# Small constant products on TensorE around the normed output stages of a two-model forward pass

## The chip, the cores and the metric

The kernel runs on one core of a Trainium2 chip. The metric is device time in microseconds of one execution. All arithmetic is float32 in and out; most products are made of three products of split halves.

## The reference

A first block (attention with compressed, selected and windowed keys, a retention branch, a squared-ReLU MLP) is followed by a two-layer model: layer 0 has an mLSTM mixer and layer 1 a softmax attention with forget gates (here "fox"), each followed by a convolved, gated feed-forward part. All on 512 rows of width 1024. The second model is where the change sits:

```python
def rmsnorm_2(x, w):
    xf = x.astype(jnp.float32)
    y = xf * lax.rsqrt(jnp.mean(xf * xf, axis=-1, keepdims=True) + EPS)
    return (y * w.astype(jnp.float32)).astype(x.dtype)

for layer in range(DEPTH_2):
    h = rmsnorm_2(x, norm_mix_pre[layer])
    y = mlstm_mixer(...) if layer < N_A_LAYERS else fox_mixer(...)
    x = x + rmsnorm_2(y, norm_mix_post[layer])
    h = rmsnorm_2(x, norm_ffn_pre[layer])
    y = conv_ffn(h, ...)
    x = x + rmsnorm_2(y, norm_ffn_post[layer])
    if layer == N_A_LAYERS - 1:
        k_sh, v_sh, c_sh = shared_kv(x, kv_norm, kv_w, kv_b_f)
```

There are four places of the form `x = x + rmsnorm_2(y, ...)`: after the mLSTM mixer, after feed-forward 0, after the fox mixer and after feed-forward 1. After each of the first three comes another norm of the new x and a projection of it.

## The kernel before, in words

Everything is kept transposed: x is eight tiles (KT = 8) of 128 features by 512 rows in `xT`. A projection (`dense`, L401) streams its weights in blocks through two slots; ScalarE rounds a block to its high part (L304), VectorE makes the low part (L313), and TensorE does three products per tile (`three_products`, L356 to L360, or tile by tile at L436, L437 and L441 in `by_tile`). Products are 128x128 by 128x512.

`run` (L362) takes a list of stages and makes one block of them: each engine goes through its own part of all stages in order, and at the end of the block every engine drains and takes part in a barrier (those instructions carry L365). The next `run` starts behind it.

The last thing in the block of each normed output stage is `post_root` (L739). The output tiles y have been squared and added on the way (`sums_on_the_way`, L691). In `post_root`, TensorE waits for the sum of seven squares and makes column means of it (`column_sums`, L570, instructions at L574), waits for the eighth square and adds its column sums; ScalarE takes the root of the 128x4 result (L754), VectorE the reciprocal (L758), and TensorE spreads the reciprocals over all partitions into `bank[6]` (`spread`, L578, instructions at L581). VectorE waits for the spread. Then the block ends.

The next block begins with `update_and_split` (L775; for feed-forward 0, fox and feed-forward 1) or, after the last stage, with `update_and_store` (L822), which has no part for TensorE. In both, VectorE scales each y tile by gain and root (`scale_tile`, L768) and adds it to `xT` (`add_tile`, L773). In `update_and_split`, ScalarE then makes the high half of the tile (L585) and its square (L788), VectorE the low half (L589), and TensorE takes the tile into the first block of the next projection (`by_tile`), with the column sums of the tile before it behind each tile's products (`sums`, called by `with_tile`, L809). The feed-forward projections have two chunks, six products for each tile; the fox one (`ff`) has one chunk, three products. ScalarE's square of tile k waits for the column sums of tile k-2, and behind the square of tile 3 ScalarE rounds the second weight block before it goes on to tile 4.

`ident_b` and `bias_b` are 128x128 bf16 constants, made at the start; the attention adds its causal bias with one product of the two at L1092.

Of the kernel before, what the change touches and what calls it, by code (L numbers as in the profile page):

```python
# [13 lines left out]
P = 128  # L14
# [165 lines left out]
def build(nc, io, at):  # L180
    top = ExitStack()
    with top:
        def sb(ctx, name, shape, dt=F32):
            return ctx.enter_context(nc.sbuf_tensor(name, shape, dt))
# [13 lines left out]
        ident_b = sb(top, "ident_b", [P, P], BF16)  # L198
        bias_b = sb(top, "bias_b", [P, P], BF16)
# [12 lines left out]
        bank = [top.enter_context(nc.psum_tensor(f"bank{i}", [P, 512], F32)) for i in range(8)]  # L212
# [357 lines left out]
        def column_sums(pe, col, src, first, last):  # L570


            for t in range(TT):
                ins = pe.matmul(bank[7][:, col + t:col + t + 1], src[:, t * P:(t + 1) * P], mean_of[:, 0:1],  # L574
                                start=first and t == 0, stop=last and t == TT - 1)
            return ins

        def spread(pe, dst, col):  # L578

            for t in range(TT):  # L580
                ins = pe.matmul(dst[:, t * P:(t + 1) * P], col[:, t:t + 1].broadcast_to([P, P]), ident, start=True, stop=True)  # L581
            return ins

        def high(act, k, vec):
            act.activation(a_hi[:, k, :], xT[:, k, :], ACT.Copy, scale=vec(k)).then_inc(split_hi_done.sem, 1)  # L585

        def low(dve, k, vec, b_hi):
            dve.wait_ge(split_hi_done.sem, b_hi + k + 1)
            dve.scalar_tensor_tensor(a_lo[:, k, :], xT[:, k, :], vec(k), a_hi[:, k, :].bitcast(F32),  # L589
                                     ALU.mult, ALU.subtract).then_inc(split_lo_done.sem, 1)  # L590

        def halves_ready(b_hi, b_lo):
            return lambda k: ((split_hi_done.sem, b_hi + k + 1), (split_lo_done.sem, b_lo + k + 1))

        def split_gained(vec):

            b_hi, b_lo, b_pr = split_hi_done.n, split_lo_done.n, products_done.n

            def scalar(act):
                act.wait_ge(products_done.sem, b_pr)  # L600
                for k in range(KT):
                    high(act, k, vec)

            def vector(dve):
                for k in range(KT):
                    low(dve, k, vec, b_hi)
            split_hi_done.n += KT
            split_lo_done.n += KT
            return {"scalar": scalar, "vector": vector}, halves_ready(b_hi, b_lo)

        def pre_root():

            b_s, b_r, b_i, b_sp = sums_ready.n, root_ready.n, inv_ready.n, spread_ready.n

            def act_part(act):
                act.wait_ge(sums_ready.sem, b_s + 1)
                act.activation(inv_col[:, :], bank[7][:, 4:4 + TT], ACT.Sqrt, bias=EPS).then_inc(root_ready.sem, 1)

            def dve_part(dve):
                dve.wait_ge(root_ready.sem, b_r + 1)  # L620
                dve.reciprocal(inv_col[:, :], inv_col[:, :]).then_inc(inv_ready.sem, 1)
                dve.wait_ge(spread_ready.sem, b_sp + 1)
                dve.tensor_copy(inv[:, :], bank[5][:, :])
                dve.drain()

            def pe_part(pe):
                pe.wait_ge(inv_ready.sem, b_i + 1)
                spread(pe, bank[5], inv_col).then_inc(spread_ready.sem, 1)
            for t in (sums_ready, root_ready, inv_ready, spread_ready):
                t.n += 1  # L630
            return act_part, dve_part, pe_part
# [107 lines left out]
        def post_root():  # L739

            b_sum, b_sq = summed.n, squared.n
            b_s, b_r, b_i, b_sp = sums_ready.n, root_ready.n, inv_ready.n, spread_ready.n

            def tensor(pe):
                pe.wait_ge(summed.sem, b_sum)
                column_sums(pe, 0, total, True, False)
                pe.wait_ge(squared.sem, b_sq)
                column_sums(pe, 0, sq[1], False, True).then_inc(sums_ready.sem, 1)
                pe.wait_ge(inv_ready.sem, b_i + 1)
                spread(pe, bank[6], post_col).then_inc(spread_ready.sem, 1)  # L750

            def scalar(act):
                act.wait_ge(sums_ready.sem, b_s + 1)
                act.activation(post_col[:, :], bank[7][:, 0:TT], ACT.Sqrt, bias=EPS).then_inc(root_ready.sem, 1)  # L754

            def vector(dve):
                dve.wait_ge(root_ready.sem, b_r + 1)
                dve.reciprocal(post_col[:, :], post_col[:, :]).then_inc(inv_ready.sem, 1)  # L758
                dve.wait_ge(spread_ready.sem, b_sp + 1)
            for t in (sums_ready, root_ready, inv_ready, spread_ready):  # L760
                t.n += 1
            return {"tensor": tensor, "scalar": scalar, "vector": vector}

        def scale_tile(dve, src, vec, k, b_sc, b_up):

            if k >= 2:
                dve.wait_ge(updated.sem, b_up + k - 1)
            dve.scalar_tensor_tensor(y_part[k % 2][:, :], src[:, k, :], gain(vec, k), bank[6][:, :],  # L768
                                     ALU.mult, ALU.mult).then_inc(scaled.sem, 1)

        def add_tile(dve, k, b_sc):
            dve.wait_ge(scaled.sem, b_sc + k + 1)
            dve.tensor_tensor(xT[:, k, :], xT[:, k, :], y_part[k % 2][:, :], ALU.add).then_inc(updated.sem, 1)  # L773

        def update_and_split(src, vec, pre):  # L775


            b_sc, b_up, b_hi, b_lo, b_sq, b_sum = scaled.n, updated.n, split_hi_done.n, split_lo_done.n, squared.n, summed.n
            act_root, dve_root, pe_root = pre_root()
            b_s = sums_ready.n - 1  # L780

            def ahead_act(act, second_block):
                for k in range(KT):
                    act.wait_ge(updated.sem, b_up + k + 1)
                    high(act, k, pre)
                    if k >= 2:
                        act.wait_ge(summed.sem, b_sum + k - 1)
                    act.activation(sq[k % 2][:, :], xT[:, k, :], ACT.Square).then_inc(squared.sem, 1)  # L788
                    if k == 3:
                        second_block()  # L790
                act_root(act)

            def ahead_dve(dve, second_block):
                for k in range(KT):
                    scale_tile(dve, src, vec, k, b_sc, b_up)
                    if k >= 1:
                        dve.wait_ge(updated.sem, b_up + k)
                        low(dve, k - 1, pre, b_hi)
                    add_tile(dve, k, b_sc)
                dve.wait_ge(updated.sem, b_up + KT)  # L800
                low(dve, KT - 1, pre, b_hi)
                second_block()
                dve_root(dve)

            def sums(pe, k):
                pe.wait_ge(squared.sem, b_sq + k + 1)
                column_sums(pe, 4, sq[k % 2], k == 0, k == KT - 1).then_inc(sums_ready.sem if k == KT - 1 else summed.sem, 1)

            def with_tile(pe, k):  # L809
                if k >= 1:  # L810
                    sums(pe, k - 1)
                if k == KT - 1:
                    sums(pe, k)
            scaled.n += KT
            updated.n += KT
            split_hi_done.n += KT
            split_lo_done.n += KT
            squared.n += KT
            summed.n += KT - 1
            return dict(ahead_act=ahead_act, ahead_dve=ahead_dve, tile_ready=halves_ready(b_hi, b_lo), with_tile=with_tile), pe_root  # L820

        def update_and_store(src, vec):  # L822
# [1214 lines left out]
        def post_norm(name, y, src=None):  # L2037

            early_dve, late_dve, late_act, count = sums_on_the_way(y, copied(y))
            stages, ready = [], None  # L2040
            if src is not None:
                stage, ready = split_tiles(src, a_hi, a_lo, KT)
                stages.append(stage)
            stages.append(dense(name, two_chunks(a_tiles), early_dve, late_dve, none, late_act, tile_ready=ready))
            count()
            run(*stages, post_root())
# [216 lines left out]
```

## Time and profile before

| | us |
|---|---|
| median of 3 runs (lowest, highest) | 2392.88 (2389.38, 2394.75) |
| the profiled execution | 2392.39 |
| its span | 2390.5 |
| mean granted TensorE clock | 0.943 |
| TensorE busy with products | 2184.3 (91%) |
| VectorE busy | 1236.5 (52%) |
| ScalarE busy | 827.9 (35%) |

The profiled execution is 1.9 us longer than its span, the time from the first to the last instruction. The granted clock is a share of 2.4 GHz: 1.0 is 2.4 GHz and 0.5 is 1.2 GHz; no other level is granted, and a mean between them is a mix.

### The profile page before, as it was taken

How to read it: one execution, taken by the hardware profiler on the slowest of the kernel's cores; microseconds unless marked ns; L12 is line 12 of the kernel's file. 1: busy time of each engine (PE TensorE's matmuls, PEld its weight loads, DVE VectorE, ACT ScalarE, POOL GpSimd, SP SyncE). 2: the span in 40 equal slices, each digit the busy share in tenths (PEclk: the TensorE clock that was granted, in tenths of full speed). 3: DMA queues.
4: the chain of work that ended last, by engine and by line, in shares of the span. 5: the costliest groups of instructions: out<-in, count | busy, mean ns of one | idle time of the engine just before them, and what ended most of it. 6: DMA issues, size and time to landing. Idle time of an engine off the chain costs nothing. (4 is left out here: it accounts for less than half of the span.)

```text
span 2390.5 us, 27004 instructions
## 1 busy us (share of the span) xinstructions
PE 2184.3 (91%) x10048; PEld 1752.7 (73%) x10048; DVE 1236.5 (52%) x1760; ACT 827.9 (35%) x1202; POOL 25.4 (1%) x50
## 2 busy tenths in 40 slices
PE   7878888999999998798699999997998789999997
PEld 6645666887888887676578888876886467888885
DVE  4566444445443455324557465556344655747465
ACT  4146214433222123224435233333124654524232
POOL 0000000000000000002000000001000000000000
PEclk9868998999999999898799999996999999999998
DMA  5200211232222321221112223212221011222221
GB/s 170 78 1 1 106 44 53 83 118 88 88 98 96 106 88 62 89 88 53 36 54 106 104 88 106 84 49 88 88 88 53 1 55 69 96 99 92 101 88 53
DMA packets 33848, 185.85 MB, mean 78 GB/s; under 512 B 4024, under 2 KB 8280, under 8 KB 14176
## 3 DMA queue, kind: packets, MB, share of 16 engines
q1 hardware_dynamic: 32608, 182.57, 21.7%
q10 hardware_dynamic: 1152, 2.10, 0.3%
q8 instruction: 56, 0.92, 0.2%
q14 instruction: 32, 0.26, 0.0%
HBM read 182.54 MB, written 2.11 MB: 77 GB/s over the span
## 5 line engine op out<-in xcount | busy, mean ns | idle before, releaser
L358 PE MATMUL bank<-a_hi,w_hi 128*128 128x512 f32 x1504 | 591.4, 393 | 29.1 <-DVE w_lo L313 23.3
L304 ACT ACTIVATE w_hi<-w_raw 128x2048 fp32r<-128x2048 f32 (+3 forms) x171 | 313.8, 1836 | 875.0 <-PE bank L360 771.5
L359 PE MATMUL bank<-a_lo,w_hi 128*128 128x512 f32 x1504 | 588.9, 392 | 0.0
L360 PE MATMUL bank<-a_hi,w_lo 128*128 128x512 f32 x1504 | 588.6, 391 | 0.0
L313 DVE TENSOR_TENSOR w_lo<-w_raw,w_hi 128x2048 fp32r<-128x2048 f32 (+3 forms) x171 | 374.9, 2193 | 191.1 <-ACT w_hi L304 191.0
L358 PEld LDWEIGHTS bank<-a_hi,w_hi 128*128 128x128 f32 x1504 | 284.8, 189 | 90.1 <-DVE w_lo L313 24.6
L360 PEld LDWEIGHTS bank<-a_hi,w_lo 128*128 128x128 f32 x1504 | 284.7, 189 | 59.9
L359 PEld LDWEIGHTS bank<-a_lo,w_hi 128*128 128x128 f32 x1504 | 284.9, 189 | 58.7
L358 PE MATMUL bank<-w_hi,a_hi 128*128 128x512 f32 (+1 forms) x288 | 111.2, 386 | 6.3 <-DVE w_lo L313 2.7
L360 PE MATMUL bank<-w_hi,a_lo 128*128 128x512 f32 (+1 forms) x288 | 109.7, 381 | 0.0
L359 PE MATMUL bank<-w_lo,a_hi 128*128 128x512 f32 (+1 forms) x288 | 109.6, 381 | 0.0
L358 PE MATMUL bank<-ffn_hi,w_hi 128*128 128x512 f32 x264 | 103.4, 392 | 3.0 <-DVE w_lo L313 3.0
L359 PE MATMUL bank<-ffn_lo,w_hi 128*128 128x512 f32 x264 | 102.8, 389 | 0.0
L360 PE MATMUL bank<-ffn_hi,w_lo 128*128 128x512 f32 x264 | 102.7, 389 | 0.0
L2085 DVE TENSOR_TENSOR ffn_u<-bank,inv 128x512 f32<-128x512 f32 x88 | 56.7, 687 | 79.6 <-PE bank L360 78.9
L436 PE MATMUL bank<-a_hi,w_hi 128*128 128x512 f32 x112 | 53.0, 473 | 36.7 <-ACT a_hi L585 14.0
L2073 ACT ACTIVATE ffn_z<-ffn_u,conv 128x512 f32<-128x512 f32 x88 | 66.5, 803 | 26.7 <-DVE ffn_u L2085 26.7
L358 PE MATMUL bank<-mlp_hi,w_hi 128*128 128x512 f32 x192 | 74.7, 389 | 0.0
L359 PE MATMUL bank<-mlp_lo,w_hi 128*128 128x512 f32 x192 | 74.7, 389 | 0.0
L360 PE MATMUL bank<-mlp_hi,w_lo 128*128 128x512 f32 x192 | 74.7, 389 | 0.0
L2076 ACT ACTIVATE ffn_z<-ffn_z 128x512 f32<-128x512 f32 x44 | 27.9, 634 | 120.8 <-DVE ffn_z L2095 120.8
L358 PEld LDWEIGHTS bank<-w_hi,a_hi 128*128 128x128 f32 x288 | 54.8, 190 | 19.2 <-issue 4.1
(367 smaller groups left out, 3016.9 us busy)
## 6 DMA issues: line engine op xcount, KB each, us to landing
w_raw<-in_w_fu SPq DMA_DIRECT2D x44, 1024.0 KB, 4.8
w_raw<-in_w_up SPq DMA_DIRECT2D x16, 1024.0 KB, 4.9
w_raw<-in_w_down SPq DMA_DIRECT2D x16, 1024.0 KB, 4.8
w_raw<-in_w_fd SPq DMA_DIRECT2D x16, 1024.0 KB, 4.8
w_raw<-in_w_mix SPq DMA_DIRECT2D x8, 1024.0 KB, 4.8
w_raw<-in_w_fd SPq DMA_DIRECT2D x8, 768.0 KB, 4.3
w_raw<-in_w_rqk SPq DMA_DIRECT2D x4, 1024.0 KB, 4.9
w_raw<-in_w_rvg SPq DMA_DIRECT2D x4, 1024.0 KB, 4.8
```

Source lines behind the costliest of these rows:

```text
L304: act.activation(w_hi[slot][:, 0:n], raw[slot][:, 0:n], ACT.Copy).then_inc(hi_ready.sem, 1)
L313: dve.tensor_tensor(w_lo[slot][:, 0:n], raw[slot][:, 0:n], w_hi[slot][:, 0:n].bitcast(F32), ALU.subtract).then_inc(lo_ready.sem, 1)
L358: pe.matmul(out, w[0], x[0], start=first, stop=False)
L359: pe.matmul(out, w[0], x[1], start=False, stop=False)
L360: return pe.matmul(out, w[1], x[0], start=False, stop=last)
L436: pe.matmul(bank[2 * slot + c][:, :], w[0], x[0], start=k == 0, stop=False)
L2073: act.activation(z[slot][:, c, :], u[slot][:, c, 2:S + 2], ACT.Identity, scale=tap(2, b, c), bias=tap(3, b, c)).then_inc(tapped.sem, 1)
L2076: act.activation(z[slot][:, 0, :], z[slot][:, 0, :], ACT.Gelu_apprx_tanh).then_inc(gelu_ready.sem, 1)
L2085: ins = dve.tensor_tensor(u[slot][:, c, 2:S + 2], bank[2 * slot + c][:, :], inv[:, :], ALU.mult)
```

## The change

A helper `keep_busy` issues n products of `ident_b` with `bias_b` (128x128 by 128x128, bf16) into `bank[4]`, which nobody reads at that point. They wait for nothing and signal nothing. `post_root` issues 7 of them between the column sums and the wait for the reciprocals, and 32 behind the spread; this is in all four normed output stages. `update_and_split` issues 12 behind the products of tile 0, in the three stages that have it. In all 4 x 39 + 3 x 12 = 192 products, each with its own weight load.

```diff
+        def keep_busy(pe, n):
+
+            for _ in range(n):
+                pe.matmul(bank[4][:, 0:P], ident_b[:, :], bias_b[:, :], start=True, stop=True)
+
@@ post_root, tensor(pe)
                 column_sums(pe, 0, total, True, False)
                 pe.wait_ge(squared.sem, b_sq)
                 column_sums(pe, 0, sq[1], False, True).then_inc(sums_ready.sem, 1)
+                keep_busy(pe, 7)
                 pe.wait_ge(inv_ready.sem, b_i + 1)
                 spread(pe, bank[6], post_col).then_inc(spread_ready.sem, 1)
+                keep_busy(pe, 32)
@@ update_and_split
             def with_tile(pe, k):
                 if k >= 1:
                     sums(pe, k - 1)
+                elif k == 0:
+                    keep_busy(pe, 12)
                 if k == KT - 1:
                     sums(pe, k)
```

## Rows read from the trace of the kernel before

**Rows 1.** The page: busy time by engine, and the granted clock in 40 slices
```profile
PE 2184.3 (91%) x10048; PEld 1752.7 (73%) x10048; DVE 1236.5 (52%) x1760; ACT 827.9 (35%) x1202; POOL 25.4 (1%) x50
...
PEclk9868998999999999898799999996999999999998
```

**Rows 2.** Timeline (start, duration in us) of the output stage after the mLSTM
```profile
1223.02 0.39 PE L360 MATMUL bank<-a_hi,w_lo 128*128 128x512 f32 x1
...
1225.70 1.65 PE L574 MATMUL bank<-mean_of,sq 128*128 128x1 f32 x8
...
1227.38 0.17 ACT L754 ACTIVATE post_col<-bank 128x4 f32<-128x4 f32 x1 [2.59 <-PE bank L574]
...
1227.82 2.08 PE L581 MATMUL bank<-const_sb,post_col 128*128 128x128 f32 x8 [0.47 <-DVE post_col L758]
```

**Rows 3.** Source view of L365, 1227 to 1232 us: ns min/median/max, first to last start
```profile
L365 PEldq EVENT_SEMAPHORE  x2: 51/51/51, 1230.0 to 1230.4; - x2
L365 DVEq EVENT_SEMAPHORE  x2: 21/21/21, 1230.2 to 1230.4; - x2
L365 POOLq EVENT_SEMAPHORE  x2: 17/17/17, 1230.3 to 1230.3; - x2
L365 PEldq DRAIN  x1: 2103/2103/2103, 1227.8 to 1227.8; - x1
```

**Rows 4.** Timeline: the first instructions behind that barrier
```profile
1230.63 0.75 DVE L768 SCALAR_TENSOR_TENSOR y_part<-y,gains,bank 128x512 f32<-128x512 f32 x1 [2.87 <-POOL ffn_u L2059]
...
1232.14 0.72 ACT L585 ACTIVATE a_hi<-xT,gains 128x512 fp32r<-128x512 f32 x1 [4.58 <-DVE xT L773]
...
1233.01 0.76 PE L436 MATMUL bank<-a_hi,w_hi 128*128 128x512 f32 x1 [3.11 <-ACT a_hi L585]
```

**Rows 5.** Windows, TensorE alone: stretch, length, busy (count), granted clock, DMA share, GB/s
```profile
1222.50:1225.50 3.00, 1.62 (x11) 1.00 0.00 0
...
1226.00:1232.50 6.50, 3.42 (x15) 0.50 0.12 21
...
1236.00:1236.50 0.50, 0.50 (x3) 0.82 0.00 0
```

**Rows 6.** Source view of L1092, the same product in the attention
```profile
L1092 PE MATMUL bank<-bias_b,ident_b x128: 219/219/314, 142.7 to 1932.9; 128*128 128x128 bf16 x128
```

**Rows 7.** Timeline of two such pairs (the first product alone, then both), and their clocks
```profile
142.74 0.29 PE L1092 MATMUL bank<-bias_b,ident_b 128*128 128x128 bf16 x1
...
142.74 0.40 PE L1092 MATMUL bank<-bias_b,ident_b 128*128 128x128 bf16 x2
...
1932.86 0.28 PE L1092 MATMUL bank<-bias_b,ident_b 128*128 128x128 bf16 x2
...
142.50:143.50 1.00, 1.00 (x10) 0.50 0.00 0
1932.50:1933.50 1.00, 1.00 (x8) 1.00 0.00 0
```

**Rows 8.** Timeline: tiles 3 and 4 of feed-forward 0's first projection
```profile
1240.59 0.63 ACT L788 ACTIVATE sq<-xT 128x512 f32<-128x512 f32 x1 [1.04 <-PE bank L574]
...
1241.13 1.89 ACT L304 ACTIVATE w_hi<-w_raw 128x2048 fp32r<-128x2048 f32 x1
...
1243.68 0.50 PE L436 MATMUL bank<-a_hi,w_hi 128*128 128x512 f32 x1 [0.86 <-ACT a_hi L585]
```

**Rows 9.** Timeline, then windows, of the fox projection's tiles
```profile
1617.39 0.80 PE L441 MATMUL bank<-a_lo,w_hi 128*128 128x512 f32 x1 [1.21 <-DVE a_lo L589]
...
1620.44 0.79 PE L436 MATMUL bank<-a_hi,w_hi 128*128 128x512 f32 x1 [2.25 <-ACT a_hi L585]
...
1639.38 0.77 PE L436 MATMUL bank<-a_hi,w_hi 128*128 128x512 f32 x1
...
1620.00:1644.00 24.00, 23.09 (x85) 0.50 0.08 26
...
1649.00:1650.00 1.00, 1.00 (x9) 0.90 0.00 0
```

## Prediction

> **What bounds the kernel now.** I read the page first: TensorE is busy 91% of the span, and its granted clock is at the full 2.4 GHz in most slices with short dips [rows 1]. So the kernel is bound by TensorE, and what is left to gain lies where it waits or runs at 1.2 GHz. The change touches four such places. I then read the timeline of the one after the mLSTM, the source view of the block end, and the clock in windows; the other three show the same pattern to a few hundredths of a microsecond.
>
> The order of events there: the last dense product starts at 1223.02; the column sums of the last square start at 1225.70; the root starts at 1227.38; the spread starts at 1227.82 and lasts 2.08 us [rows 2]. TensorE's clock is still full up to 1225.5 and is at half from 1226.0, so the sums of the last square and the spread run at 1.2 GHz [rows 5]. It rises again inside 1236.0 to 1236.5, some 3 us after the first dense products of the next projection began at 1233.01 [rows 4, 5].
>
> What matters most is what stands between the spread and the next work. TensorE's queue has a DRAIN of 2.103 us that begins at 1227.8 and so ends at 1229.9, with the spread. Its barrier semaphore follows at 1230.0, VectorE's at 1230.2, GpSimd's at 1230.3 [rows 3]. Only behind that barrier does VectorE scale the first tile, at 1230.63, ScalarE makes its high half at 1232.14 and TensorE starts on it at 1233.01 [rows 4]. The source view shows the same 2.103 us drain at all three places where another projection follows, and at the last place too. So whatever TensorE has in its queue ahead of the block's end holds up every engine, and VectorE's chain behind the barrier is the critical path: TensorE itself is idle for 3.11 us waiting for it [rows 4].
>
> **The change part by part.**
>
> *The price of one product.* The kernel already has the same product, one at a time 0.219 us long at the full clock [rows 6]. Two in a row last 0.28 us at the full clock, so the second adds 0.06; at half clock one lasts 0.29 and two 0.40, so the second adds 0.11 [rows 7]. I take 0.11 and 0.06. Only pairs are in the trace: if a longer row did not overlap at all, each would cost up to the 0.31 us of the longest single one [rows 6], which I hold for unlikely, since a pair overlaps.
>
> *7 products behind the column sums.* They come after the clock has fallen, so they can't keep it up. They fill the 0.47 us in which TensorE waits for root and reciprocal [rows 2]: 7 x 0.11 = 0.77 us. The last column sum starts about 0.35 us before its end, so the products get perhaps 0.15 us more than the gap. Bounds per place: 0 (all hidden) and 0.3 (nothing but the gap). I take 0.15; four places, 0.6 us.
>
> *32 products behind the spread.* These stand ahead of the block's DRAIN. The cover would be the wait of 3.11 us for the first tile, but that wait only begins when the barrier is through: the products don't lie beside it, they push it back. 32 x 0.11 = 3.5 us, if the clock stays at half. Off that go 0.2 us, the time by which TensorE's semaphore is ahead of VectorE's now [rows 3], and some 0.3 us because TensorE is then continuously busy for over 5 us and the clock, which rose about 3 us after dense work began [rows 4, 5], should rise near the end of the row. That leaves 3.0 us at each of four places, 12.0 us. Bounds: all 32 at the full clock, 32 x 0.06 - 0.2 = 1.7 us, and all at half with no rise, 3.5 - 0.2 = 3.3 us; times four, 6.8 and 13.2.
>
> *What the risen clock brings.* After the products TensorE waits again, now for barrier, two VectorE and one ScalarE instruction: 1229.9 to 1233.01, 3.1 us, unchanged in length. The trace shows that the clock fell within 2.6 us after the last dense product, although the first column sums lay in that time [rows 2, 5]. An idle wait of 3.1 us should lose it again, before or about when tile 0 arrives. Then tiles 0 and 1 run at 1.2 GHz as now. Gain taken: 0. If the clock is full for tile 0: TensorE is late in this stretch, ScalarE's square of tile 3 waits 1.04 us for its column sums, the weight block is rounded behind that, and tile 4 starts on TensorE behind both [rows 8]. With a full clock nearly all of that goes; about 0.9 us at each of the two feed-forward stages.
>
> The Trainium skill ("TensorE: Matmul & The Clock Gate", section on HAM oscillation) says that bursts of products with waits between them start at the low clock again each time, because the clock is released by recent activity and throttled by recent idleness. By that rule the 32 products buy a clock which the wait behind them gives back. No row here shows such a burst of small products; if the page's opposite advice, keep TensorE busy before dense work, decided instead, the sum would be that of the rival "clock is kept" below.
>
> *12 products behind tile 0.* In the feed-forward stages, TensorE goes from tile 0 to tile 1 with no wait at half clock, so 12 products cost up to 12 x 0.11 = 1.3 us there, less what an earlier rise of the clock or a later wait takes back (ScalarE's waits for sums pass a delay on to tile 4). Bounds: -0.9 us (clock full, the products in a gap, the gain above) and +1.3 us. I take 0.4 at each of two stages, 0.8 us. In the fox stage they are hidden: TensorE waits 2.25 us before tile 1 [rows 9], because VectorE is slow there.
>
> *Sum.* 0.6 + 12.0 + 0.8 = 13.4 us on the profiled execution's 2392.39 (span 2390.5 and 1.9 outside it) gives 2405.8. The median of the runs is 0.5 above the profiled one, so 2406.
>
> **The rivals.**
>
> *The clock is not down when the products come.* The time that passes before the clock falls need not be the same at every place once the first one has moved the rest. If it stays full through sums and spread at a place, the spread costs about 1 us less and the 32 products only 1.7 us: about +1 us there. If this held at three of four places: 3.2 + 3 x 1 = 6, less up to 1.8 at the tiles, some +4 us, 2397. For it: the fall now comes right inside the sums, a small shift could move it. Against: all four places of before, hundreds of microseconds apart, fall at the same point.
>
> *The clock is kept (not slower).* If the products raise the clock early and it survives the wait, the fox stage decides: now its clock is at half from the output stage to 1649 us [rows 9]; tiles 1 to 7 start 18.94 us apart in all, 3.2 us a tile, and at the full clock VectorE's three instructions a tile, 0.75 us for the longest [rows 4], some 2.2 in all, would set the pace. Six tiles give 5.6 us; of the ten us from 1639.4 until the clock has risen at 1649.5, all TensorE's at half clock, I estimate that a third would go, 3.4, so 9 us; with 1.8 in the feed-forward stages that is 11 against 4 x 1.7 + 0.6 = 7.4: -3.5 us, 2389. Its place is the fox projection, its price 9 us, and it decides if the clock is full when tile 1 of fox arrives. Against it: after tile 0 in fox TensorE has waits of over 1 and over 2 us between few products [rows 9], and 12 products of 0.06 cover 0.7 of them.
>
> *The drain does not hold the others.* If the 32 products ran beside the barrier, they would end about when tile 0 arrives and cost nothing, the clock would be up for the feed-forward tiles: -1.8 + 0.6, down to -10 with fox: 2382 to 2391. Against it stands the 2.103 us DRAIN that ends with the spread [rows 3].
>
> **How the numbers follow.** The sum as worked out 0.78, clock not down 0.12, clock kept 0.05, drain doesn't hold 0.05. The likeliest gives 2406; its own range is 2398 to 2410: 6.8 us less 1.8 at the tiles is +5, and 13.2 with 1.2 and 2.6 for the other two parts is +17. For 8 in 10 I go down into the first rival and up for products that overlap less than the pairs do: 2397 to 2411. A measurement of this kernel tells 0.2%, 4.8 us, from no change. Slower by more: the likeliest case and a part of the first rival, 0.82. Within: the rest of the first rival and most of the clock kept, 0.12. Faster: 0.06.
>
> **What would show it.** In the profile after, the DRAIN of TensorE in front of each of the four barriers is some 5.3 us long in place of 2.1; VectorE's first scaling starts 3 us later after the reciprocal than now; the last place shows the same loss though no product follows it. The 32 products take 3 to 3.5 us, most at 0.5. The clock is at half when tile 0's products start, and fox's tiles still run at half to the end. The prediction is wrong if the scaling follows the spread as soon as before, if the products run at 0.06 us each, or if the fox tiles run at the full clock.

## The result, and the profile after

The changed kernel takes 2405.86 us (median of 12 runs, 2403.59 to 2416.74), the kernel before 2392.35 (median of 12, 2389.38 to 2401.11): ratio 1.0060, 95% interval 1.0044 to 1.0077. It is 13.5 us slower; 13.4 had been forecast on the profiled execution.

The profiled execution of the changed kernel is a long one, 2416.27 us with a span of 2414.5. Of the 24 us by which its span exceeds the one before, 8.25 were there before the first changed instruction ran: the first output stage's root starts at 1235.63, before at 1227.38 [rows 2]. A second profile of the same program (below, `changed_again`) has that root at 1226.09 and a span of 2403.3. So I measure from root to root and not from the span's start; what the 8.25 us consist of is in the last section. The page of the first profile, to be held against [rows 1]:

```profile
PE 2210.7 (92%) x10240; PEld 1772.8 (73%) x10240; DVE 1236.3 (51%) x1760; ACT 827.8 (34%) x1202; POOL 25.4 (1%) x50
```

TensorE has its 192 more products, and nothing else in the counts has moved. The page alone doesn't tell where the time went. The timeline of the first output stage does (start, duration in us, what; idle time ahead of it in brackets), against [rows 2, 4]:

```profile
1235.46 0.55 PE L587 MATMUL bank<-bias_b,ident_b 128*128 128x128 bf16 x7
1235.63 0.17 ACT L761 ACTIVATE post_col<-bank 128x4 f32<-128x4 f32 x1 [1.97 <-PE bank L574]
...
1236.07 2.08 PE L581 MATMUL bank<-const_sb,post_col 128*128 128x128 f32 x8
1237.94 2.66 PE L587 MATMUL bank<-bias_b,ident_b 128*128 128x128 bf16 x32
...
1241.15 0.75 DVE L775 SCALAR_TENSOR_TENSOR y_part<-y,gains,bank 128x512 f32<-128x512 f32 x1 [5.14 <-POOL ffn_u L2068]
...
1242.66 0.72 ACT L590 ACTIVATE a_hi<-xT,gains 128x512 fp32r<-128x512 f32 x1 [6.86 <-DVE xT L780]
...
1243.53 0.77 PE L436 MATMUL bank<-a_hi,w_hi 128*128 128x512 f32 x1 [2.93 <-ACT a_hi L590]
```

The 32 products stand between the spread and the first scaling. The spread is over by 1238.15, yet VectorE scales only at 1241.15, half a microsecond behind the last product, and TensorE then waits 2.93 us for tile 0, as it waited 3.11 before. The source view of the block's end in the same stretch (ns min/median/max, first to last start), against [rows 3]:

```profile
L365 DVEq EVENT_SEMAPHORE  x2: 21/21/21, 1238.5 to 1240.9; - x2
L365 PEldq EVENT_SEMAPHORE  x2: 51/51/51, 1240.7 to 1240.9; - x2
L365 PEldq DRAIN  x1: 1170/1170/1170, 1239.5 to 1239.5; - x1
```

TensorE's drain ends at 1240.7, behind the last product's end at 1240.60, and its semaphore follows at once. VectorE had reached its own semaphore at 1238.5, so it stood at the barrier for 2.2 us until TensorE came; before, TensorE's semaphore at 1230.0 was ahead of VectorE's at 1230.2 [rows 3]. The granted clock over the same stage, in windows of TensorE alone (stretch, length, busy, clock, DMA share, GB/s), against [rows 5]:

```profile
1235.50:1236.00 0.50, 0.50 (x8) 1.00 0.00 0
1236.50:1239.00 2.50, 2.50 (x18) 0.50 0.00 0
1239.50:1240.00 0.50, 0.50 (x13) 1.00 0.00 0
1240.00:1242.50 2.50, 0.60 (x11) 1.00 0.10 13
1243.00:1249.00 6.00, 5.47 (x22) 0.50 0.38 158
1249.50:1250.00 0.50, 0.50 (x5) 0.84 0.00 0
```

The products did raise the clock, between 1239.0 and 1239.5. Then TensorE was idle until 1243.53, and the clock was at half again when tile 0 arrived; it came back six microseconds into the tiles. In that time stand the 12 products and what follows from them:

```profile
1246.23 1.50 PE L587 MATMUL bank<-bias_b,ident_b 128*128 128x128 bf16 x12
...
1250.94 0.63 ACT L795 ACTIVATE sq<-xT 128x512 f32<-128x512 f32 x1 [3.12 <-PE bank L574]
...
1256.34 0.50 PE L436 MATMUL bank<-a_hi,w_hi 128*128 128x512 f32 x1 [0.86 <-ACT a_hi L590]
```

They ran at half clock and held tile 1 back until 1247.49; ScalarE's square of tile 2 waited 3.12 us for column sums, and tile 4 starts 15.19 us behind the first scaling, before 13.05 [rows 4, 8].

The same intervals at all places and in all kernels that were run, one profile each, worked out from the timelines (us, each from start to start; the four places are the output stages after the mLSTM, feed-forward 0, fox, feed-forward 1):

| kernel | root to first scaling, the four | scaling to tile 4's high half, ffn 0 and 1 | scaling to tile 7's, fox | root to root | last root to end |
|---|---|---|---|---|---|
| before | 3.25 3.05 3.25 3.05 | 12.29 12.37 | 24.49 | 382.18 382.20 382.16 | 16.58 |
| changed | 5.52 5.14 6.33 5.71 | 14.43 13.15 | 24.47 | 385.99 387.17 386.47 | 19.24 |
| changed_again | 6.36 5.73 6.26 5.65 | 13.15 13.16 | 24.48 | 386.49 385.11 386.47 | 19.14 |
| only_32 | 6.40 6.23 6.17 6.23 | 12.38 12.40 | 24.48 | 385.20 386.68 385.02 | 19.77 |
| only_12 | 3.25 2.13 3.19 3.06 | 12.99 14.00 | 24.48 | 382.38 383.55 383.54 | 16.61 |
| only_7 | 3.28 3.09 3.28 3.09 | 12.30 12.38 | 24.48 | 382.22 382.24 382.20 | 16.59 |
| moved_32 | 3.28 2.22 3.28 3.07 | 13.61 12.26 | 24.46 | 383.03 381.07 381.62 | 16.65 |
| double_32 | 8.15 5.46 7.77 7.05 | 11.60 12.85 | 24.49 | 385.86 386.35 386.68 | 20.62 |
| before_sums | 2.33 3.05 3.25 3.05 | 13.00 13.13 | 24.49 | 381.40 381.96 382.45 | 16.54 |
| all_gaps | 2.34 2.13 3.25 2.46 | 11.61 12.33 | 24.48 | 380.03 383.37 381.64 | 15.97 |
| fox_fill | 2.34 2.24 2.33 2.14 | 11.59 11.63 | 21.86 | 380.08 374.21 380.00 | 15.69 |
| fox_only | 3.25 3.05 3.25 3.05 | 12.34 12.38 | 21.85 | 382.20 375.45 382.14 | 16.56 |

The first three columns are the stages themselves. A root to root holds some 350 us of other work besides, in which the granted clock dips at other moments in each execution, and the middle one moves most by it. The changed kernel has 387.17 there in one profile and 385.11 in the other, though the first of the two had the shorter time from the second root to the first scaling (5.14 us against 5.73). In only_12, from the first scaling to the third root, TensorE is busy 338.42 us at a mean clock of 0.92, before 335.24 at 0.93. So a difference of 1 or 2 us in the middle column, in a single profile, isn't to be read as an effect.

### The profile page after: what moved, and what is told of

Read it like the earlier page. It is cut to its first block and busy times, and to the rows that moved or that the text cites. A ratio compares the mean times of both kernels' runs of the same rounds, so it can differ in the third digit from the quotient of the medians.

```text
span 2414.5 us, 27388 instructions
## 1 busy us (share of the span) xinstructions
PE 2210.7 (92%) x10240; PEld 1772.8 (73%) x10240; DVE 1236.3 (51%) x1760; ACT 827.8 (34%) x1202; POOL 25.4 (1%) x50
```

## The experiments

The theory: TensorE's drain and the barrier at the block's end wait for all that TensorE has been given, so 32 products ahead of it are paid in full at four places. The rivals: the 12 products are the larger cost; the 192 products cost wherever they stand; the clock is what decides. Medians are of 4 to 12 runs of each kernel beside 29 runs of the kernel before, but fox_only and changed_again ran once.

### Each part alone

```diff
 # only_32: the 7 and the 12 are taken out
-                keep_busy(pe, 7)
...
-                elif k == 0:
-                    keep_busy(pe, 12)
```

> Only the 32 products behind the spread, no 7 and no 12. Theory (the drain at the block's end holds every engine): from the root to the first scaling 5.2 to 6.3 us in place of 3.05 to 3.25 at each of four places, the tiles behind it paced as before, in all +9 to +12 us on the median of the kernel before. Rival 1 (the 12 products behind tile 0 are the larger cost): under +5 us. Rival 2 (the products run beside the barrier): the time from root to scaling stays at 3.2 us, and the total at that of before.

Measured 2405.01 us against 2392.3, ratio 1.0055 (1.0041 to 1.0069): 12.7 us, nearly the whole loss, from the 32 alone, and slightly more than the 9 to 12 expected. From root to scaling 6.17 to 6.40 us, 12.4 us more than before at the four places together. Its timeline at the first place, then its clock in windows:

```profile
1228.93 3.54 PE L587 MATMUL bank<-bias_b,ident_b 128*128 128x128 bf16 x32
...
1233.03 0.75 DVE L774 SCALAR_TENSOR_TENSOR y_part<-y,gains,bank 128x512 f32<-128x512 f32 x1 [6.01 <-POOL ffn_u L2065]
...
1235.40 0.53 PE L436 MATMUL bank<-a_hi,w_hi 128*128 128x512 f32 x1 [2.92 <-ACT a_hi L590]
```

```profile
1232.00:1235.00 3.00, 0.48 (x6) 0.96 0.35 44
1235.50:1236.00 0.50, 0.50 (x2) 0.67 1.08 459
1236.00:1239.00 3.00, 3.00 (x8) 0.50 0.41 175
```

Here one sees the purchase and its loss: the clock is full from about 1232 to 1235.5, in which TensorE has next to nothing to do. It falls just when tile 0 has started: its first product still lasts 0.53 us, before 0.76 [rows 4], and everything in the three microseconds behind runs at half. Tile 4 gains nothing by it (12.38 us, before 12.29). The last stage is the cleanest place of all, since no product follows it: last root to end 19.77 us in place of 16.58.

```diff
 # only_12: the 7 and the 32 are taken out
-                keep_busy(pe, 7)
...
-                keep_busy(pe, 32)
```

> Only the 12 products behind tile 0. Theory: they are run at half clock and push tile 1 back; ScalarE's squares pass that on, so in the two feed-forward stages tile 4 comes 0.7 to 2.1 us later after the first scaling than the 12.3 us of before, in fox not at all; in all +1.5 to +4 us. Rival (the products raise the clock for the tiles, as they are meant to): tile 4 at 12.3 us or earlier, total the same or a little less.

Measured 2394.74 us, ratio 1.0004 (0.9992 to 1.0016), which can't be told from no change. The profile can: tile 4 is 0.70 and 1.63 us later than before in the two feed-forward stages, and fox's tiles are where they were. That is within what the theory expected. At the first place the 12 themselves last 1.03 us, at the other two 1.50. One root to scaling is 2.13 us and its spread 1.16 us long: the clock had not fallen there yet, which gives part of the cost back.

```diff
 # only_7: the 32 and the 12 are taken out
-                keep_busy(pe, 32)
...
-                elif k == 0:
-                    keep_busy(pe, 12)
```

> Only the 7 products between column sums and spread. Theory: 0.15 us at each of four places, from root to scaling 3.2 to 3.4 us, total within 1 us of before. Rival (they also keep the clock up for the spread): the spread lasts 1.05 us in place of 2.08 at one or more places, total 1 to 4 us less.

Measured 2391.79 us, ratio 1.0001 (0.9987 to 1.0014). From root to scaling 0.03 to 0.04 us more than before, at all four places.

```profile
1225.27 0.91 PE L587 MATMUL bank<-bias_b,ident_b 128*128 128x128 bf16 x7
1225.45 0.17 ACT L760 ACTIVATE post_col<-bank 128x4 f32<-128x4 f32 x1 [2.55 <-PE bank L574]
...
1225.97 2.02 PE L581 MATMUL bank<-const_sb,post_col 128*128 128x128 f32 x8
```

The spread starts 0.52 us behind the root in place of 0.44 and is 0.06 shorter. Neither a cost nor a clock.

### The same 32, behind the barrier

```diff
 # moved_32
                     tiles = len(sets[0])
+                    if with_tile is not None:
+                        with_tile(pe, -1)
...
-                keep_busy(pe, 32)
...
             def with_tile(pe, k):
+                if k == -1:
+                    keep_busy(pe, 32)
```

> The change whole, but with the 32 products behind the barrier, ahead of the wait for tile 0, in the three stages that have it. Theory (the barrier makes the cost): from root to scaling back to 3.2 to 3.4 us; tile 0 starts on TensorE at most 1 us late if the products run at half clock (32 x 0.107 = 3.4 us against 2.4 us of waiting), and the clock is full at tile 0 or 1. In all -2 to +3 us against before, 10 us or more under the changed kernel. Rival (192 more products and their instructions cost wherever they stand): within 3 us of the changed kernel.

Measured 2391.41 us, ratio 0.9999 (0.9985 to 1.0013), 14 us under the changed kernel: 0.9 less than the kernel before that ran beside it, where the changed one took 13.5 more. This tells the theory from the rival of "wherever they stand", as 96 of the 128 products are still there (the last stage has no tiles for its 32). Its timeline:

```profile
1228.61 0.75 DVE L776 SCALAR_TENSOR_TENSOR y_part<-y,gains,bank 128x512 f32<-128x512 f32 x1 [2.90 <-POOL ffn_u L2071]
1228.63 3.57 PE L589 MATMUL bank<-bias_b,ident_b 128*128 128x128 bf16 x32 [0.75 <-PEq L365]
...
1231.96 0.77 PE L438 MATMUL bank<-a_hi,w_hi 128*128 128x512 f32 x1
```

Scaling and products now start together. At half clock the products outlast the wait: tile 0 starts 3.35 us behind the first scaling, before 2.38 [rows 4], its first product is still at half clock (0.77 us), and with the 12 behind it tile 4 comes 1.32 us later than before. At the other two places the clock rose during the row: tile 0 starts at 3.05 and 3.06 us and its first product lasts 0.48 and 0.47. So the move takes the cost at the drain away, and what is left of it at the tiles is about made up elsewhere (root to scaling of 2.22 us at one place).

### Twice as many

```diff
 # double_32: only these, and 64
-                keep_busy(pe, 32)
+                keep_busy(pe, 64)
```

> Only the products behind the spread, but 64. Theory (all that stands ahead of the drain is paid): the second 32 run at the full clock, 0.056 us each, so 1.8 us more than with 32 alone at each of four places: root to scaling 7.9 to 8.3 us, +7 us against 32 alone. Rival (the cost is a fixed one of a risen clock or of a longer program): the same as with 32 alone.

Measured 2409.08 us, ratio 1.0079 (1.0051 to 1.0107): 4 us more than with 32 (4.6 if each is taken against the kernel before that ran beside it), where 7 were expected. The cost grows with the number, as for work that is paid, but less than forecast. At the first place it is the sum expected:

```profile
1227.79 5.29 PE L587 MATMUL bank<-bias_b,ident_b 128*128 128x128 bf16 x64
...
1233.64 0.75 DVE L774 SCALAR_TENSOR_TENSOR y_part<-y,gains,bank 128x512 f32<-128x512 f32 x1 [7.77 <-POOL ffn_u L2065]
...
1236.02 0.47 PE L436 MATMUL bank<-a_hi,w_hi 128*128 128x512 f32 x1 [2.93 <-ACT a_hi L590]
```

At the second, all ran at the full clock (spread 1.16 us, the 64 products 3.74, root to scaling 5.46), and at the other two it rose earlier in the row (4.91 and 4.45 us). The expected 7 us had the first 32 cost as much as in only_32, mostly at half clock, everywhere. And at the first the clock lived through the wait: tile 0's first product lasts 0.47 us, not 0.76 [rows 4], and tile 4 comes 0.69 us earlier than before. So a risen clock is not always lost in a wait of 2.9 us: in only_32 it fell as tile 0 started, here it did not. At the third place it was full at tile 0 as well (0.47 us), but at half again from 2009.4 on, 1.5 us into the tiles, and tile 4's high half came at 12.85 us, later than before (12.37). A full clock at the first product isn't enough.

### Products where they stand beside a wait

```diff
 # before_sums: the 7, 32 and 12 are taken out
             def tensor(pe):
+                keep_busy(pe, 24)
                 pe.wait_ge(summed.sem, b_sum)
```

> No 7, 32 or 12; in their place 24 products ahead of the wait for the sum of squares, where TensorE waits 1.38 us at the full clock, in all four stages. Theory (the clock falls because of that wait, and products help only where they stand beside a wait that nothing queued behind them delays): the last column sums 1.03 and the spread 1.1 us long in place of 1.5 to 1.65 and 2.08, root to scaling 2.1 to 2.3 us; -1.6 us a place, in all -4 to -6.5 us. Rival (24 small products are too few to keep the clock): the same as before.

Measured 2390.55 us, ratio 0.9986 (0.9969 to 1.0003): a gain at the edge of what can be measured, and less than was expected. The column sums run at the full clock everywhere (1.03 us), but the spread only at the first place (1.16 us); at the other three it is 2.08 as before. The clock fell a little later, in front of the spread. In both feed-forward stages tile 4 came 0.7 us later than before, which takes part of the gain back. The fall was delayed, not prevented, so half of the theory held.

```diff
 # all_gaps: as before_sums, with the 7, and
             def with_tile(pe, k):
+                if k == -1:
+                    keep_busy(pe, 36)
```

> 24 products ahead of the sum of squares, 7 before the reciprocals, 36 behind the barrier ahead of tile 0; none ahead of the drain, none behind tile 0. Theory: clock full from the sums on, spread about 1.1 us, tile 0 on TensorE at 2.4 us after the first scaling and at the full clock; tile 4's high half 11.4 to 12.3 us after the first scaling in the feed-forward stages. In all -5 to -8 us. Rival (a full clock at tile 0 brings nothing, as in the run with 32 alone): only the -4 to -6.5 us of the spread and sums.

Measured 2388.39 us, ratio 0.9979 (0.9967 to 0.9991). That is 3.4 us under the kernel before, less than the 5 to 8 expected. Where the clock held (feed-forward 0), tile 0 starts at 2.28 us and tile 4 comes 0.68 us earlier than before. Where it was down again when the 36 ran (fox and feed-forward 1), they outlast the wait: tile 0 at 3.39 and 3.77 us.

```diff
 # fox_fill: as all_gaps, and in the fox projection
+                if vec == 9 and 0 <= k < KT - 1:
+                    keep_busy(pe, 36 if k == 0 else 8)
```

> As all_gaps, and in the fox projection 36 products behind tile 0 and 8 behind each of tiles 1 to 6. Theory: if these keep the clock full through fox's tiles, tile 7's high half comes at 21 to 22.5 us after the first scaling in place of 24.5, and the stage ends 7 to 9 us earlier: -12 to -16 us in all. Rival (waits of over 1 us between tile 0's products lose the clock first, and the added products then run at half): fox later than before by 0 to 8 us.

Measured 2378.13 us, ratio 0.9952 (0.9931 to 0.9973): 13.7 us under the kernel before, the best of all that were run. Its timeline in the fox stage, and its clock:

```profile
1611.24 0.75 DVE L777 SCALAR_TENSOR_TENSOR y_part<-y,gains,bank 128x512 f32<-128x512 f32 x1 [1.85 <-PEq L365]
1611.39 3.29 PE L589 MATMUL bank<-bias_b,ident_b 128*128 128x128 bf16 x36 [0.69 <-PEq L365]
...
1614.49 0.48 PE L438 MATMUL bank<-a_hi,w_hi 128*128 128x512 f32 x1
...
1616.35 2.19 PE L589 MATMUL bank<-bias_b,ident_b 128*128 128x128 bf16 x36
...
1619.06 0.50 PE L438 MATMUL bank<-a_hi,w_hi 128*128 128x512 f32 x1 [0.52 <-ACT a_hi L592]
```

```profile
1616.00:1626.00 10.00, 8.66 (x85) 1.00 0.23 95
1626.00:1640.00 14.00, 13.40 (x96) 0.92 0.14 47
```

Before, the clock was at half from 1620 to 1644 [rows 9]. Now it is full at tile 0 and through the tiles (the 0.92 is a fall behind the last tile; from 1616.0 to 1637.5 the windows give 1.00). The second to third root takes 374.21 us in place of 382.20, and each root to root around a feed-forward stage 2.1 to 2.2 us less than before. The 8.0 us around fox are 0.8 from root to scaling, 2.6 up to tile 7's high half, and 4.6 behind it, where before TensorE still ran at half clock (1636.0 to 1649.0: 13.00 us busy of 13.00 at 0.50). The first tiles gained nothing: the high half of tile 3 comes at 12.15 us, before 12.24, and that of tile 4 at 15.23, before 17.02.

```diff
 # fox_only: of fox_fill only what stands in fox's projection
-                keep_busy(pe, 24)
...
-                keep_busy(pe, 7)
...
-                if k == -1:
+                if k == -1 and vec == 9:
                     keep_busy(pe, 36)
```

> Only the fox projection is filled: 36 products behind the barrier, 36 behind tile 0, 8 behind each of tiles 1 to 6; nothing at the column sums or in the feed-forward stages. Theory: the clock is at half when the 36 begin; they run 2 to 3.9 us and raise it by tile 1, so tile 7's high half comes at 21.8 to 23 us after the first scaling in place of 24.5; second to third root 375 to 378 us in place of 382.2. Rival (the clock must be kept from the sums on): 381 us or more.

One run, 2384.12 us beside 2391.62. Second to third root 375.45 us, so most of the 8.0 us of fox_fill comes from what stands in fox's projection, with the clock at half when the 36 begin (0.50 from 1607.0 to 1613.0, 1.00 from 1614.0 to 1637.0). The 2.64 us up to tile 7 are sure, as all profiles without this filling have 24.46 to 24.49; the 4.1 behind it, from a single profile, carry the wander of that stretch. The two feed-forward intervals are those of before.

### The changed kernel once more

```diff
 # changed_again: no difference
```

> The changed kernel once more, for a second profile. In its first profile the root of the first output stage came 8.25 us later than before, ahead of anything that was changed. If that is the wander of one execution: here it comes at 1225 to 1230 us, as in the other kernels, and the time is near 2406. If it belongs to the changed kernel: again near 1235 and the time near 2414. From root to root 3.5 to 5 us more than the 382.2 of before in either case.

2405.31 us, and the first root at 1226.09: the 8.25 us ahead of the change were that one execution's. From root to root it is 4.3, 2.9 and 4.3 us more than before; the second is under the 3.5 to 5 expected. Its timeline shows the 32 at the first place nearly all at half clock:

```profile
1225.91 0.91 PE L587 MATMUL bank<-bias_b,ident_b 128*128 128x128 bf16 x7
...
1228.43 3.46 PE L587 MATMUL bank<-bias_b,ident_b 128*128 128x128 bf16 x32
...
1232.45 0.75 DVE L775 SCALAR_TENSOR_TENSOR y_part<-y,gains,bank 128x512 f32<-128x512 f32 x1 [5.97 <-POOL ffn_u L2068]
```

## Why the prediction was right, step by step

**The 32 products (12.0 us, at 3.0 a place).** Right in mechanism and size. In `changed_again`, root to scaling grew by 3.11, 2.68, 3.01 and 2.60, 11.4 us with the 7 in it; in the first profile by 2.27, 2.09, 3.08 and 2.66, 10.1; in only_32 it is 12.4. The spread between executions is that of the clock: the row of 32 lasts 2.53 or 2.66 us where it rises half way and 3.5 where it doesn't. The price per product from pairs [rows 7] was right: 3.54 us for 32 is 0.11 each.

**The 7 products (0.6 us).** Off by the size: 0.03 to 0.04 a place, 0.1 in all. The estimated tail behind the last column sum was too careful; the spread starts 0.08 us later and is 0.06 shorter.

**What the risen clock brings (0).** Right in the sum, and only in part by the way forecast. At the first two places of the first profile the clock was at half again before tile 0 (first product 0.77 and 0.76 us). In only_32 and `changed_again` it was still full when tile 0 started, at all three places, and fell during or within 1 us of the first product, which lasts 0.47 to 0.74 us. The tiles behind ran at half either way, so tile 4 gained nothing (12.38 and 12.40 us in only_32). As a rule it is too strong: in double_32, at the first place, the clock lived through the wait and the tiles. The gain of a full clock at tile 0, put at 0.9 us, is 0.7 where it stays full up to tile 4 (double_32, all_gaps and fox_fill, first place).

**The 12 products (0.8 us).** Too low: 0.86 and 0.79 us in `changed_again`, 2.14 and 0.78 in the first profile, 0.70 and 1.63 alone. I had weighed the gain of a clock that wasn't full against the cost, and the cost is the nearer end. In fox they were hidden, as said.

**Sum.** 11.4 and 1.65 us of `changed_again` are 13.1; from its first root to its end it is 14.1 us longer than before, against 13.4 forecast. Of the remaining 1.0, 0.7 are the last column sums ahead of the second, third and fourth root, which are 0.25, 0.13 and 0.36 us longer than before (1.84, 1.67 and 1.84 us); why they were slower was not followed. That the total came within 0.1 us of the forecast is luck: the 32 and the 7 cost about 1.2 us less than forecast, the 12 and the column sums about 1.6 more, and the first profile's four places gave 10.1 where the second's gave 11.4.

**The rivals.** "The drain does not hold the others" fell with moved_32. "The clock is not down" happened at single places (the second in only_12, moved_32 and double_32), never at all four. "The clock is kept" named the right place and about the right price, 9 us for fox, where fox_fill measures 8.0 from root to root. It is not the same sum, though: 5.6 us were forecast for the tiles and 3.4 behind them, and 2.6 and 4.6 were measured: the high halves of tiles 1 to 3 came no sooner at the full clock. The change has 12 products there; fox_only did it with 120, and no number between was tried.

**The checks that failed.** The 32 products were to take 3 to 3.5 us; they took 2.53 to 3.44 in the first profile and 3.01 to 3.46 in the second. I had also said that the drain's record would be 5.3 us long in place of 2.1. It is 1.17 us, and 1.95 at the third place. Its end is where it was forecast, behind the last product; its start is not. At 1239.5, where the record begins, 16 of the 32 products have yet to start; in double_32 it begins with 18 of the 64 yet to start, and is again 1.17 us long. So the length of a drain is no measure of what it waits for. What decides when the record begins is not shown.

## What to carry to other kernels

Fill a wait with extra products only where nothing else waits for what stands behind them in the queue: put them behind the barrier, not ahead of it. Then fill until the awaited work arrives, and look in the clock windows of the trace whether the clock is full at that moment and stays so through the tiles behind. The place with the most to gain here was the longest stretch at half clock (fox, 40 us): 120 products around and between its tiles gave 6.75 us in one profile, about half of what the best kernel gained in all.

## What the runs showed that was not expected

The same program's first output stage came at 1226.09 in one execution and at 1235.63 in another, 9.5 us apart, with nothing changed ahead of it. Up to that root TensorE was busy 1101.33 us in the slower one, at a mean granted clock of 0.92, and 1093.58 us in the other, at 0.93, while VectorE (580.14 and 580.20) and ScalarE (390.73 and 390.65) did the same in the same time. So 7.75 of the 9.5 us are the same products at a lower clock. Why the clock was lower more of the time in one execution is open.

Products ahead of the sum of squares put the clock's fall off without preventing it: with 24 of them the column sums ran at the full clock at four places of four, and the spread at one of four. With products in the other gaps too (all_gaps) it was two of four, and with fox's tiles filled (fox_fill) all four, at 1.16 to 1.26 us, though the two programs do the same from the fox tiles' end to the next spread. Whether the place in time decides this, or what went before, is open.
